# Second part of the conditioning as row sums on VectorE, with the loads, the second z unit and the first fox product reordered

## Chip, cores, metric

One core of one Trainium2 chip. The metric is the device time of the program in microseconds (us), the median of several executions. The engines are TensorE (PE, with its weight loads PEld), VectorE (DVE), ScalarE (ACT), GpSimd (POOL) and SyncE (SP), which here only issues loads.

## The reference

One decoder layer on 256 tokens of width 1024, all in float32. What matters here:

```
mod = (c @ w_ada + b_ada).reshape(B, 6, D)        # w_ada is 1024 x 6144
h = rms_norm(x, g1) * (1 + sc1) + sh1
dn_qkv, dn_z, dn_b, dn_a, fx_qkv, fx_f, gate_a, gate_b = split(h @ w_in)
y_a = (rms_norm(gated_delta_rule(...)) * silu(dn_z)) @ w_o_delta
y_b = forgetting_attention(...) @ w_o_fox
x = x + gt1 * ((sigmoid(gate_a) * y_a + sigmoid(gate_b) * y_b) @ w_out)
h2 = rms_norm(x, g2) * (1 + sc2) + sh2
x = x + gt2 * moe_ffn(h2, ...)                     # 32 experts, top 4
```

`mod` is a product of one row, `c`, with a matrix of 24 MB, called the conditioning below. It is used in three parts of two vectors each: part 0 (sh1, sc1) at the start, part 1 (gt1, sh2) and part 2 (sc2, gt2) after the mixers.

## The kernel before

Every weight before the experts passes through a ring of 8 slots of 1 MB in SBUF. The list UNITS gives the order of the units of 1 MB; unit n goes to slot n % 8, and SP issues its load as soon as unit n - 8 has been used. SP takes the list in order, so a unit whose slot isn't free holds back all behind it. Names: `ada0`, `ada1`, `ada2` are the three parts of the conditioning (8 units each), `dn` the DeltaNet projections (6), `fqk` q and k of the fox attention (4), `fv` its v (2), `z` (2), `gates` (8), then the output matrices.

A projection unit of `w_in` (from `dn` 1 on) is split into a rounded high part and a low part, half a unit (m = 0, 1) at a time: ACT copies the high part (L1130, `split_hi`), POOL subtracts to get the low part (L1846), and PE multiplies in three passes (`three_passes`). ACT splits two units ahead of the one that it takes out of PSUM: in `take(name, u)` the split of a later unit stands in front of the copy of this one, so `fv` 0 is split ahead of the copy of `fqk` 2, of the exponential `exg` (L1196) and of the split of `fv` 1. HI_BUF gives two buffers in turn for the high parts. For `fv` PE waits for both halves before it starts.

The conditioning is computed in two ways. Parts 0 and 1: PE multiplies each unit by `c`, repeated over 32 columns (`ada`, 4 products of 512 columns a unit), and a unit counts as used when PE is done with it. Part 2 (SUMMED): DVE adds the rows weighted by `c` (`add_rows`, L1428 for k = 0, L1431 for the others), each unit being added onto the sum that stands in the unit before; then PE adds over the 128 partitions with 4 products (`ada_over_rows`). There unit k counts as used only when the sum k + 1 is done (`ada_added`), since that sum reads it. Both leave a row in a PSUM bank, which DVE copies (`take_mod_rows`, L1406), PE transposes (`mod_transposes`, L531 to L538), and DVE adds to the biases (`take_mod`, L1390 to L1397).

PE's order around the change is: `fqk` 3, sums of squares for k, `fv` 0 and 1, transposes of k (L704) and of v (L710), `z` 0 and 1, the pair products k k and k q (`chunk_pairs`, 64 x 64), the 8 units of `ada(1, 5)`, `mod_transposes(1, 6)`, transposes of the first inverse (L727), `gates` 0, and five levels of inversion between the halves of `gates` 1 to 5. Then follows the recurrence over four chunks, in which fox products (`fox_branch`) fill gaps, and `fox_branch(2)` behind it, which waits until DVE has taken the first fox group (`take_yb(0)`, L1625). DVE's order is: convolutions of the six `dn` units, small vectors, four pairs of forget-gate masks (L1482, L1484, `rowF_taken`), normalising q and k (L1494, L1496), decays (L1503, L1504), the copies kbx, kd, vb (L1515), the pair products' matrix (L1531), level 0 (L1537), first inverse (L1542).

Of the kernel before, what the change touches and what calls it, by code (L numbers as in the profile page):

```python
# [15 lines left out]
ALU = mybir.AluOpType  # L16
# [24 lines left out]
def layer_kernel(nc, x, c, w_ada, b_ada, g_norm1, w_in, conv_w, a_log, dt_bias, g_onorm, b_fgate,  # L41
# [3 lines left out]
    KD = D // P  # L45
# [18 lines left out]
    W = H * HD  # L64
    COL_Z = QKV
    COL_SMALL = COL_Z + W
    COL_FOX = COL_SMALL + 2 * H
# [4 lines left out]
    with ExitStack() as ctx:  # L72
# [17 lines left out]
        def S(name):  # L90
            if name not in sems:
                sems[name] = ctx.enter_context(nc.semaphore(name))
            return sems[name]
# [160 lines left out]
        def bank(b, a=0, n=512):  # L254
            return ps[:, b, a:a + n]
# [13 lines left out]
        def ada_part(part, ks=range(KD)):  # L269
            return [(f"ada{part}", k, ada_unit(part, k)) for k in ks]  # L270

        def win_part(name, col, us):
            return [(name, u, win_unit(col + 256 * u)) for u in us]

        UNITS = ada_part(0) + win_part("dn", 0, range(6))
        UNITS += win_part("fqk", COL_FOX, range(4)) + win_part("fv", COL_FOX + 2 * W, (0, 1))
        UNITS += win_part("z", COL_Z, (0, 1)) + ada_part(1)
        UNITS += win_part("gates", COL_GATES, range(5)) + ada_part(2, range(3))
        UNITS += win_part("gates", COL_GATES, range(5, 8)) + ada_part(2, range(3, KD))
        UNITS += [("wo_fox", u, rows_unit(w_o_fox, 256 * u, 2)) for u in range(2)]  # L280
# [1 line left out]
        UNITS += [("w_out", u, rows_unit(w_out, 256 * u, 2)) for u in range(4)]  # L282
        NUNITS = len(UNITS)
        UNIT_AT = {(name, i): n for n, (name, i, _) in enumerate(UNITS)}
        SUMMED = (2,)
        SUMMED_NAMES = [f"ada{part}" for part in SUMMED]
        USED_AT = {}
        for name, i, _ in UNITS:
# [215 lines left out]
        def _(pe):  # L504
# [12 lines left out]
            def ada(part, b, ks=range(KD)):  # L517

                for k in ks:
                    w = unit_arrived(pe, f"ada{part}", k)  # L520
                    for q in range(4):
                        last = mm(ps[32 * q:32 * q + 32, b, :], cb[:, k, :], w[:, 512 * q:512 * q + 512],
                                  k == 0, k == KD - 1)
                    last.then_inc(S("unit_used"), 1)
# [102 lines left out]
            def project(name, u, ms=(0, 1)):  # L627


                n = nproj[0]  # L630
                b = n % 2
                if (name, u) in SPLIT:
                    last = project_split(name, u, ms)
                    if ms[-1] == 1:
                        last.then_inc(S("unit_used"), 1)
                        nproj[0] += 1
                    return
                w = unit_arrived(pe, name, u).rearrange("p (k n) -> p k n", k=KD)
                if ms[0] == 0 and n >= 2:
                    bank_free(n)  # L640
                for m in ms:
                    for k in range(KD):
                        if n == 0 and m == 0 and k % 4 == 0:
                            pe.wait_ge(S("hT_low" if k == 0 else "hT_high"), 1)
                        lhsT, rhs = w[:, k, m * P:(m + 1) * P], (hT_first if n < WHOLE else hT)[:, k, :]
                        last = mm(bank(b, m * T, T), lhsT, rhs, k == 0, k == KD - 1)
                if ms[-1] == 1:
                    last.then_inc(S("unit_used"), 1)
                    nproj[0] += 1
# [58 lines left out]
            for t in range(TT):  # L708
                for h in range(H):
                    last = pe.transpose(bank(3 + t, h * P, P), vT[:, h, t * P:(t + 1) * P], ident)  # L710
            last.then_inc(S("tok_ps"), 1)
            project("z", 0)
            project("z", 1)

            pe.wait_ge(S("tok_taken"), 1)
            chunk_pairs((2, 7), kn, kn).then_inc(S("pairs_ps"), 1)
            pe.wait_ge(S("tok_taken"), 2)
            pe.wait_ge(S("unit_qk"), 1)
            chunk_pairs((3, 4), kn, qn).then_inc(S("pairs_ps"), 1)
            pe.wait_ge(S("rowF_taken"), 1)  # L720
            ada(1, 5)
            mod_transposes(1, 6)

            pe.wait_ge(S("X1_ready"), 1)
# [639 lines left out]
        def _(dve):  # L1364
# [69 lines left out]
            for u in range(6):  # L1434
                dve.wait_ge(S("unit_used"), USED_AT[("dn", u)])
                for back in range(4):
                    for m in (2 * u, 2 * u + 1):
                        w = vec("conv", 12 * (3 - back) + m)
                        drawn = bank(u % 2, (m % 2) * T, T - back)
                        if back == 0:  # L1440
                            last = TS(qkv[:, m, :], drawn, w, None, ALU.mult)
                        else:
                            last = STT(qkv[:, m, back:T], drawn, w, qkv[:, m, back:T], ALU.mult, ALU.add)
                    if back < 3:
                        link(last)
                last.then_inc(S("conv_ready"), 1)
            dve.wait_ge(S("conv_ready"), 6)

            dve.wait_ge(S("small_ps"), 2)
# [30 lines left out]
            for h in range(H):  # L1480
# [3 lines left out]
                last = STT(fox_e1[:, h, :], bank(b, a, T), cums[:, 2, 1, H + h:H + h + 1], em("fox_open", 2 * P),  # L1484
                           ALU.subtract, ALU.add)
            last.then_inc(S("rowF_taken"), 1)
            dve.wait_ge(S("rowF_taken"), 1)

            for half in range(2):
# [34 lines left out]
            for t in range(TT):  # L1524
                last = per_head(vb[:, t], 3 + t, beta[:, t, :])
            last.then_inc(S("tok_taken"), 1)
            dve.wait_ge(S("pairs_ps"), 1)
            dve.wait_ge(S("decay_ready"), 1)
            for t in range(TT):
# [18 lines left out]
                last = TTn(attn_t[:, t], bank(3 + t).rearrange("p (h n) -> p h n", h=H), dec_a[:, t], ALU.mult)  # L1548
            last.then_inc(S("attn_ready"), 1)
            TTn(qn, qn, exg, ALU.mult).then_inc(S("qd_ready"), 1)  # L1550
            take_mod_rows(1, 5)
            take_mod(1, 6)
            dve.wait_ge(S("U1_ps"), 1)
            CP(Um[:, 0], bank(2).rearrange("p (h n) -> p h n", h=H))
# [1 line left out]
            for s in range(1, LEVELS):  # L1556
# [30 lines left out]
                if s == 3:  # L1587
# [3 lines left out]
                    TTn(fox_p1, fox_p1, fsum[:, 1, :].unsqueeze(2).to_broadcast([P, H, T]), ALU.mult).then_inc(  # L1591
                        S("fox_p_ready"), 1)

            add_rows(2, 3)
            dve.wait_ge(S("M_ready"), LEVELS - 1)
            dve.wait_ge(S("uw_ps"), 1)
# [2 lines left out]
            for n in range(NCH):  # L1599
                t, r = n // 2, (n % 2) * CH  # L1600
                rows = slice(r, r + CH)
                if n > 0:
                    dve.wait_ge(S("ws_ps"), n)
                    TTn(vnew[rows, t], u_sb[rows, t], ps[rows, 2, :].rearrange("p (h n) -> p h n", h=H),
                        ALU.subtract).then_inc(S("vnew_ready"), 1)
                if n < 2:
                    add_rows(2, 4 + 2 * n)
                if n < NCH - 1:
                    dve.wait_ge(S("ds_ps"), n + 1)
                    if n == 0:  # L1610
                        last = CP(state, bank(7).rearrange("p (h n) -> p h n", h=H))
                    else:
                        for h in range(H):
                            last = STT(state[:, h, :], state[:, h, :], eg[:, h, n:n + 1], bank(7, h * P, P),
                                       ALU.mult, ALU.add)
                    last.then_inc(S("state_ready"), 1)
                    if n < 2:
                        add_rows(2, 5 + 2 * n)
                    dve.wait_ge(S("state_ready"), n + 1)
            take_mod_rows(2, 6)  # L1620

            def take_yb(g):
                dve.wait_ge(S("yb_ps"), g + 1)
                gb_ms = gates[:, 8 + 2 * g:10 + 2 * g, :]
                TTn(gb_ms, bank(g % 2).rearrange("p (m n) -> p m n", m=2), gb_ms, ALU.mult).then_inc(S("yb_taken"), 1)  # L1625

            take_yb(0)
            take_yb(1)
            take_mod(2, 6)
            STT(A2_runs, A2_runs, 1.0, run_vecs[:, 8:12, :].rearrange("p r k -> p (r k)"), ALU.add, ALU.mult)  # L1630
# [286 lines left out]
```

## Time and profile before

| | us |
|---|---|
| median of 3 runs | 1228.27 (1225.92 to 1231.68) |
| the profiled execution | 1225.72 |
| its span, first to last instruction | 1223.9 |
| PE busy in the span | 1130.1 |
| DVE, ACT, POOL busy | 337.1, 185.5, 108.8 |

The time of the profiled execution is 1.8 us more than its span. The change lies in the first 256 us; from about 300 us on the experts run. Times in the rows below are us from the start of the span.

### The profile page before, as it was taken

To read this page: it belongs to the slowest core of one execution; us is meant where nothing else is said; L and a number is where in the kernel's file an instruction comes from. 1 tells how busy PE (TensorE), PEld (TensorE's weight loads), DVE (VectorE), ACT (ScalarE), POOL (GpSimd) and SP (SyncE) were. 2 spreads that over 40 slices of the span, in tenths; PEclk is the share of its full clock that TensorE was granted. 3 is DMA by queue.
4 is the path that set the end of the run, shared out by engine and by line. 5 is a ranking of instruction groups with operands and counts; after the bars stand their busy time and mean duration, and the time that the engine had idled before them with its cause. 6 is when DMAs were issued, how large, how long until landed. Compare 5 with 4: busy or idle time off the path is not lost.

```text
span 1223.9 us, 15032 instructions
## 1 busy us (share of the span) xinstructions
PE 1130.1 (92%) x6251; PEld 582.7 (48%) x6251; DVE 337.1 (28%) x682; ACT 185.5 (15%) x317; POOL 108.8 (9%) x50
## 2 busy tenths in 40 slices
PE   5999999999999999988989889999999999989886
PEld 2999799878433434433333333333433433333322
DVE  1633557341422121321221212122122312212102
ACT  2465344001200000100000000000001000000002
POOL 0764444020000000000000000000000000000000
PEclk9999999999999999999999999999999999999999
DMA  9973765498999999999999999999999999999995
GB/s 352 340 224 103 241 238 207 132 369 333 418 421 428 427 428 428 428 428 428 428 428 428 428 428 428 428 428 428 428 429 428 428 428 428 428 428 428 428 427 245
DMA packets 62559, 464.71 MB, mean 380 GB/s; under 512 B 8469, under 2 KB 31130, under 8 KB 34618
## 3 DMA queue, kind: packets, MB, share of 16 engines
q1 hardware_dynamic: 61688, 462.92, 92.0%
q10 hardware_dynamic: 786, 1.14, 0.3%
q8 instruction: 26, 0.43, 0.1%
q0 software_dynamic: 48, 0.13, 0.0%
q14 instruction: 11, 0.09, 0.0%
HBM read 463.13 MB, written 1.05 MB: 379 GB/s over the span
## 4 chain that ended last, share of the span: by engine, by line
PE 68%; DMA 24%; issue 2%; DVE 2%; ACT 2%; SPq 0%; POOL 0%; DVEq 0%; ACTq 0%
PE ps L506 65%; DMA ring<-in_w_down_dram 12%; DMA ring<-in_w_gate_up_dram 6%; DMA kept<-in_w_down_dram 4%; DMA ring<-in_w_ada_dram 2%; PE ps L973 1%; ACT kept L1324 1%; POOL w_lo L1846 0%; PE ps L1005 0%; ACT w_hi L1130 0%; SPq L350 0%; DVE ring L1537 0%; DVE ring L1531 0%; PE ps L533 0%; DVE kept L1406 0%
## 5 line engine op out<-in xcount | busy, mean ns | idle before, releaser
L506 PE MATMUL ps<-ring,kept 128*64 128x512 f32 (+2 forms) x2984 | 651.3, 599 | 34.8 <-DMA ring<-in_w_down_dram 17.7
L506 PEld LDWEIGHTS ps<-ring,kept 128*64 128x64 f32 (+2 forms) x2984 | 210.5, 138 | 449.5 <-issue 397.0
L506 PE MATMUL ps<-kept 128*128 128x128 f32 (+4 forms) x984 | 192.2, 408 | 8.3 <-ACT kept L1324 3.3
L506 PEld LDWEIGHTS ps<-kept 128*128 128x128 f32 (+2 forms) x984 | 108.3, 176 | 94.5 <-issue 81.8
L1320 ACT ACTIVATE kept<-kept 128x512 f32<-128x512 f32 x32 | 20.2, 630 | 727.7 <-DVE kept L1748 727.7
L1748 DVE TENSOR_SCALAR kept<-ps 128x512 f32<-128x512 f32 x32 | 22.1, 692 | 385.9 <-PE ps L506 385.9
L1770 DVE TENSOR_TENSOR kept<-ps,kept 64x512 f32<-64x512 f32 x64 | 44.1, 689 | 293.8 <-PE ps L506 292.8
L1846 POOL TENSOR_TENSOR w_lo<-ring,w_hi 128x1024 fp32r<-128x1024 f32 x38 | 94.6, 2508 | 107.4 <-ACT w_hi L1130 107.4
L506 PE MATMUL ps<-hT_hi,w_hi 128*128 128x256 f32 x272 | 78.5, 289 | 0.4 <-POOL w_lo L1846 0.4
L506 PE MATMUL ps<-hT_lo,w_hi 128*128 128x256 f32 x272 | 76.9, 283 | 0.0
L506 PE MATMUL ps<-hT_hi,w_lo 128*128 128x256 f32 x272 | 76.8, 282 | 0.0
L506 PE MATMUL ps<-ring 64*64 64x64 f32 (+6 forms) x784 | 73.3, 267 | 1.5 <-DVE ring L1625 1.5
L506 PEld LDWEIGHTS ps<-ring 64*64 64x64 f32 (+3 forms) x784 | 64.1, 157 | 9.9 <-DVE ring L1625 2.4
L506 PE MATMUL ps<-kept,ring 128*128 128x256 f32 (+1 forms) x252 | 56.4, 381 | 4.0 <-DVE kept L1470 2.1
L506 PEld LDWEIGHTS ps<-kept,ring 128*128 128x128 f32 x252 | 47.3, 196 | 11.8 <-issue 3.3
L506 PEld LDWEIGHTS ps<-hT_hi,w_hi 128*128 128x128 f32 x272 | 52.0, 191 | 1.1 <-POOL w_lo L1846 0.6
L506 PEld LDWEIGHTS ps<-hT_lo,w_hi 128*128 128x128 f32 x272 | 52.0, 191 | 0.1
L506 PEld LDWEIGHTS ps<-hT_hi,w_lo 128*128 128x128 f32 x272 | 52.0, 191 | 0.0
L1130 ACT ACTIVATE w_hi<-ring 128x1024 fp32r<-128x1024 f32 x38 | 39.2, 1053 | 48.2 <-PE ps L506 36.9
L973 PE MATMUL ps<-kept 128*128 128x128 f32 x128 | 21.7, 292 | 22.6 <-issue 22.6
L973 PEld LDWEIGHTS ps<-kept 128*128 128x128 f32 x128 | 19.1, 206 | 33.4 <-issue 29.5
L1324 ACT ACTIVATE kept<-ps 128x512 f32<-128x512 f32 x32 | 19.1, 598 | 85.6 <-PE ps L973 85.6
(231 smaller groups left out, 536.5 us busy)
## 6 DMA issues: line engine op xcount, KB each, us to landing
ring<-in_w_gate_up_dram SPq DMA_DIRECT2D x127, 2048.0 KB, 27.6
ring<-in_w_down_dram SPq DMA_DIRECT2D x47, 2048.0 KB, 23.5
kept<-in_w_down_dram SPq DMA_DIRECT2D x16, 2048.0 KB, 24.5
ring<-in_w_ada_dram SPq DMA_DIRECT2D x24, 1024.0 KB, 7.1
ring<-in_w_in_dram SPq DMA_DIRECT2D x22, 1024.0 KB, 10.1
ring<-in_w_out_dram SPq DMA_DIRECT2D x4, 1024.0 KB, 13.7
ring<-in_w_o_fox_dram SPq DMA_DIRECT2D x2, 1024.0 KB, 6.3
ring<-in_w_o_delta_dram SPq DMA_DIRECT2D x2, 1024.0 KB, 7.7
```

Of the source, the lines that this page charges most:

```text
L506: return pe.matmul(dst, lhsT, rhs, start=start, stop=stop, skip_group_check=True)
L973: last = pe.transpose(bank(7, kk * P, P), fours[:, kk, :], ident)
L1130: A(hi_buf_r(n)[:, :, cols], w[:, :, cols], ACT.Copy).then_inc(S("split_hi"), 1)
L1320: A(sig_a, gate_a, ACT.Sigmoid, scale=ALPHA).then_inc(S("sig_ready"), 1)
L1324: A(act_t_last if par == 0 and not more else act_t, bank(7), ACT.Copy).then_inc(S("act_t_ready"), 1)
L1748: TS(gate_a, bank(4), LIMIT, None, ALU.min).then_inc(S("gate_up_taken"), 1)
L1770: TTn(ypair[par * 64:par * 64 + 64, d * 512:(d + 1) * 512], ps[64 * d:64 * d + 64, b, :], gt2_row[64 * d:64 * d + 64, d * 512:(d + 1) * 51 ...
L1846: pool.tensor_tensor(lo_r[:, :, cols], lo[:, :, cols], hi_buf_r(n)[:, :, cols].bitcast(F32), ALU.subtract).then_inc(S("split_lo"), 1)
```

## The change

Part 1 of the conditioning joins part 2 in SUMMED: 8 `add_rows` on DVE and one `ada_over_rows` on PE in place of 8 units of `ada(1, 5)`. Sums 0 to 2 stand behind the convolutions of `dn` 3, 4 and 5; sums 3 to 7 stand behind the masks that end in `rowF_taken`. The list UNITS is reordered, with the `ada1` units among and ahead of the `fqk` units, and `fv` and `z` behind them. On PE, `ada_over_rows(1, 5)` stands ahead of `z` 0, and `z` 1 behind the pair products. On DVE, `take_mod_rows(1, 5)` moves ahead of the pair products' matrix, and `take_yb(0)` into the recurrence, behind the state of the third chunk.

```diff
-        UNITS += win_part("fqk", COL_FOX, range(4)) + win_part("fv", COL_FOX + 2 * W, (0, 1))
-        UNITS += win_part("z", COL_Z, (0, 1)) + ada_part(1)
+        UNITS += ada_part(1, (0, 1)) + win_part("fqk", COL_FOX, (0, 1)) + ada_part(1, (2, 3))
+        UNITS += win_part("fqk", COL_FOX, (2,)) + ada_part(1, (4,)) + win_part("fqk", COL_FOX, (3,))
+        UNITS += ada_part(1, (5, 6, 7)) + win_part("fv", COL_FOX + 2 * W, (0, 1)) + win_part("z", COL_Z, (0, 1))
...
-        SUMMED = (2,)
+        SUMMED = (1, 2)
...
             last.then_inc(S("tok_ps"), 1)
+            ada_over_rows(1, 5)
             project("z", 0)
-            project("z", 1)
...
             chunk_pairs((3, 4), kn, qn).then_inc(S("pairs_ps"), 1)
-            pe.wait_ge(S("rowF_taken"), 1)
-            ada(1, 5)
+            project("z", 1)
             mod_transposes(1, 6)
...
                 last.then_inc(S("conv_ready"), 1)
+                if u >= 3:
+                    add_rows(1, u - 3)
...
             last.then_inc(S("rowF_taken"), 1)
+            for k in range(3, KD):
+                add_rows(1, k)
...
             last.then_inc(S("tok_taken"), 1)
+            take_mod_rows(1, 5)
             dve.wait_ge(S("pairs_ps"), 1)
...
             TTn(qn, qn, exg, ALU.mult).then_inc(S("qd_ready"), 1)
-            take_mod_rows(1, 5)
             take_mod(1, 6)
...
                     if n < 2:
                         add_rows(2, 5 + 2 * n)
+                    else:
+                        take_yb(0)
                     dve.wait_ge(S("state_ready"), n + 1)
             take_mod_rows(2, 6)
...
-            take_yb(0)
             take_yb(1)
```

Three places of the order. First SP's queue behind the small loads (`ring<-in_w_ada_dram` is a unit of the conditioning, `ring<-in_w_in_dram` a projection unit; `unit_used` is PE done with a unit, `ada_added` a sum done). Before:

```order
L350 DMA ring<-in_w_in_dram 128x8x256 [waits unit_used] x8
L350 DMA ring<-in_w_ada_dram 128x2048 [waits unit_used] x8
L350 DMA ring<-in_w_in_dram 128x8x256 [waits unit_used] x5
L350 DMA ring<-in_w_ada_dram 128x2048 [waits unit_used] x3
L350 DMA ring<-in_w_in_dram 128x8x256 [waits unit_used] x3
```

And now:

```order
L351 DMA ring<-in_w_ada_dram 128x2048 [waits unit_used] x2
L351 DMA ring<-in_w_in_dram 128x8x256 [waits unit_used] x2
L351 DMA ring<-in_w_ada_dram 128x2048 [waits unit_used] x2
L351 DMA ring<-in_w_in_dram 128x8x256 [waits unit_used]
L351 DMA ring<-in_w_ada_dram 128x2048 [waits unit_used]
L351 DMA ring<-in_w_in_dram 128x8x256 [waits ada_added]
L351 DMA ring<-in_w_ada_dram 128x2048 [waits ada_added]
L351 DMA ring<-in_w_ada_dram 128x2048 [waits unit_used] x2
L351 DMA ring<-in_w_in_dram 128x8x256 [waits ada_added] x2
L351 DMA ring<-in_w_in_dram 128x8x256 [waits unit_used]
```

The sixth row is `fqk` 3, the seventh `ada1` 5, the eighth `ada1` 6 and 7, the ninth `fv` 0 and 1, the tenth `z` 0. The loads of `fv` 0 and 1, which stood fifth and sixth of the first eight and waited for PE's use of `dn` 2 and 3, now stand behind all of `ada1`, and wait for the sums 3 and 4.

Second DVE, from the last pair of masks on, now:

```order
L1484 SCALAR_TENSOR_TENSOR kept<-ps,kept,ring 128x128
L1486 SCALAR_TENSOR_TENSOR kept<-ps,kept,ring 128x256
L1431 SCALAR_TENSOR_TENSOR ring<-ring,kept 128x2048 [waits ada_added,slot_in3]
L1431 SCALAR_TENSOR_TENSOR ring<-ring,kept 128x2048 [waits ada_added,slot_in5]
L1431 SCALAR_TENSOR_TENSOR ring<-ring,kept 128x2048 [waits ada_added,slot_in7]
L1431 SCALAR_TENSOR_TENSOR ring<-ring,kept 128x2048 [waits ada_added,slot_in0]
L1431 SCALAR_TENSOR_TENSOR ring<-ring,kept 128x2048 [waits ada_added,slot_in1]
L1498 SCALAR_TENSOR_TENSOR ring<-ring 128x1024 [waits qk_rstd,rowF_taken]
L1500 TENSOR_TENSOR ring<-ring 128x1024 [waits qk_rstd]
```

Before, the row of L1498 (then L1494) followed the masks at once; five sums now stand between them.

Third PE, behind the transposes of k and v (L705 and L711, before L704 and L710), now:

```order
L705 MATMUL ps<-kept,ring 128x128 x7
L711 MATMUL ps<-kept,ring 128x128 [waits exg_ready,dec_ready]
L711 MATMUL ps<-kept,ring 128x128 x7
L507 MATMUL ps<-ring,kept 32x512 [waits ada_added]
L507 MATMUL ps<-ring,kept 32x512 x3
```

and, behind `z` 1, which ends with three passes of the last k:

```order
L507 MATMUL ps<-hT_lo,w_hi_54 128x256
L507 MATMUL ps<-hT_hi,w_lo_62 128x256
L532 MATMUL ps<-kept 128x12 [waits run_in,mod_rows_sb]
L532 MATMUL ps<-kept 128x12
L534 MATMUL ps<-kept 128x128 x4
L539 MATMUL ps<-kept 128x64 x4
L727 MATMUL ps<-kept,ring 128x128 [waits X1_ready]
```

The 32 products of 512 columns that stood ahead of the first of these transposes (L531 before) are gone; four of them stand behind L711, and `z` 1 is what PE does ahead of the transposes.

## Rows read from the trace of the kernel before

**Rows 1.** The page: span, and GB/s in 40 slices of the span.

```profile
span 1223.9 us, 15032 instructions
...
GB/s 352 340 224 103 241 238 207 132 369 333 418 421 428 427 428 428 428 428 428 428 428 428 428 428 428 428 428 428 428 429 428 428 428 428 428 428 428 428 427 245
```

**Rows 2.** Chain that ended last, 100 to 150 us: start, us, what.

```profile
124.57 12.62 PE ps L506 x128
...
137.21 2.17 DVE ring L1531 x8
...
139.41 1.30 DVE ring L1537 x2
...
145.68 0.61 DVE kept L1406
```

**Rows 3.** Timeline of PE, 108 to 150 us: start, us, what, idle before.

```profile
109.37 0.47 PE L506 MATMUL ps<-w_hi,hT_hi 128*128 128x256 f32 x1
...
123.48 1.09 PE L710 MATMUL ps<-kept,ring 128*128 128x128 f32 x8 [1.37 <-DVE ring L1504]
...
136.01 2.08 PE L506 MATMUL ps<-ring 128*64 128x64 f32 x64
138.03 7.07 PE L506 MATMUL ps<-ring,kept 128*32 128x512 f32 x64
146.34 0.41 PE L531 MATMUL ps<-kept 12*128 12x12 f32 x2 [1.24 <-DVE kept L1406]
...
147.88 1.09 PE L727 MATMUL ps<-kept,ring 128*128 128x128 f32 x8
```

**Rows 4.** Timeline of DVE.

```profile
102.86 0.47 DVE L1484 SCALAR_TENSOR_TENSOR kept<-ps,kept,ring 128x256 f32<-128x256 f32 x1
116.80 1.23 DVE L1494 SCALAR_TENSOR_TENSOR ring<-ring 128x1024 f32<-128x1024 f32 x1 [13.47 <-ACT ring L1207]
...
178.29 3.52 DVE L1537 TENSOR_TENSOR ring<-ring 128x512 f32<-128x512 f32 x2 [0.84 <-PE ps L506]
...
195.41 4.82 DVE L1431 SCALAR_TENSOR_TENSOR ring<-ring,kept 128x2048 f32<-128x2048 f32 x2
```

**Rows 5.** DMA issues from 166 to 171 us, and from 176 to 181 us: count, size, us to landing.

```profile
ring<-in_w_in_dram SPq DMA_DIRECT2D x1, 1024.0 KB, 5.3
...
ring<-in_w_in_dram SPq DMA_DIRECT2D x1, 1024.0 KB, 6.4
```

**Rows 6.** Timeline of ACT, 108 to 116 us.

```profile
108.09 2.00 ACT L1130 ACTIVATE w_hi<-ring 128x1024 fp32r<-128x1024 f32 x2 [8.87 <-PE ps L506]
110.00 0.58 ACT L1164 ACTIVATE ring<-ps 128x512 f32<-128x512 f32 x1
...
115.63 2.01 ACT L1207 ACTIVATE ring<-ring 128x1024 f32<-128x1024 f32 x2
```

**Rows 7.** Timeline of POOL.

```profile
77.36 2.39 POOL L1846 TENSOR_TENSOR w_lo<-ring,w_hi 128x1024 fp32r<-128x1024 f32 x1 [3.54 <-ACT w_hi L1130]
...
178.83 5.21 POOL L1846 TENSOR_TENSOR w_lo<-ring,w_hi 128x1024 fp32r<-128x1024 f32 x2 [4.02 <-ACT w_hi L1130]
...
198.02 4.42 POOL L1846 TENSOR_TENSOR w_lo<-ring,w_hi 128x1024 fp32r<-128x1024 f32 x1 [3.91 <-ACT w_hi L1130]
```

**Rows 8.** Windows: length, busy of each engine (instructions), granted clock, DMA.

```profile
32.30:36.20 3.90, 3.87 (x9) 3.19 (x10) 1.29 (x1) 3.49 (x5) 0.00 (x0) 0.50 1.10 352
36.20:41.00 4.80, 4.80 (x23) 4.20 (x23) 4.77 (x3) 3.01 (x4) 4.66 (x2) 1.00 1.10 348
90.60:92.70 2.10, 0.03 (x2) 0.05 (x1) 2.03 (x4) 2.10 (x3) 1.62 (x1) 1.00 0.52 98
...
94.20:97.60 3.40, 3.40 (x17) 3.40 (x17) 0.21 (x1) 1.72 (x2) 3.40 (x2) 0.50 0.16 67
```

**Rows 9.** Timeline of PE at the end of the recurrence.

```profile
245.47 1.07 PE L506 MATMUL ps<-ring,kept 128*32 128x512 f32 x8
248.07 3.72 PE L506 MATMUL ps<-ring 128*128 128x256 f32 x16 [1.54 <-DVE ring L1625]
```

More of the change, by code:

```diff
@@ L1592, in _, with take_yb @@
                         S("fox_p_ready"), 1)
+            def take_yb(g):
+                dve.wait_ge(S("yb_ps"), g + 1)
+                gb_ms = gates[:, 8 + 2 * g:10 + 2 * g, :]
+                TTn(gb_ms, bank(g % 2).rearrange("p (m n) -> p m n", m=2), gb_ms, ALU.mult).then_inc(S("yb_taken"), 1)
             add_rows(2, 3)
@@ L1618, in _ @@
                         add_rows(2, 5 + 2 * n)
+                    else:
+                        take_yb(0)
                     dve.wait_ge(S("state_ready"), n + 1)
             take_mod_rows(2, 6)
[L1622 to L1625, printed above, removed]
-            take_yb(0)
             take_yb(1)
```

## The prediction

> **What bounds the kernel now.** I read the page first [rows 1]: from the eleventh slice on (306 us) the core moves up to 428 GB/s without a break, so the experts run at the rate of their loads. These loads are released by PE's products at the end of the mixers, so a shift of the mixers' end moves all that follows by the same. I therefore sum up shifts of PE before 256 us and take them over to the end one to one.
>
> Next the chain [rows 2]. PE holds it nearly everywhere. Between 137.2 and 146.3 us it leaves PE: the pair products release DVE, which makes the matrix (2.17), level 0 (1.30) and more, and takes the conditioning's row last (145.68, 0.61). PE's timeline shows what PE did meanwhile [rows 3]: from 138.03 it ran 7.07 us of `ada(1, 5)`, which DVE's work covers in full, and it waited 1.24 us more for the row. So removing 7.07 us of PE work alone gives nothing there; putting `z` 1 in its place does.
>
> Then who feeds PE from 103 us on. DVE ends the masks at 102.86 + 0.47 = 103.3 and idles 13.47 us, until ACT's L1207 [rows 4]; the five sums now stand in that hole. ACT splits `fv` 1 at 108.09 (`fv` 0 long before) and PE starts `fv` 0 at 109.37 without a wait [rows 3, 6].
>
> **The change, part by part.**
>
> *PE's stretch from L710's end to L727.* Before, 147.88 - (123.48 + 1.09) = 23.3 us [rows 3]. Now `ada_over_rows` (1.07, as the same four products of part 2 [rows 9]), `z` 0, pair products (2.1), `z` 1, transposes of the conditioning (147.88 - 146.34 = 1.5). A `z` unit takes (136.01 - 124.57) / 2 = 5.7 [rows 3]. Sum 1.1 + 5.7 + 2.1 + 5.7 + 1.5 = 16.1. DVE's path behind the first pair products up to the first inverse is 2.17 + 1.30 and a further pair of that length, 4.8 us [rows 2], less than `z` 1, so it is covered. Term: -7.2. Without that cover it would cost the rest of 4.8 us.
>
> *Sums 0 to 2 behind the convolutions.* A sum is 4.82 / 2 = 2.4 us [rows 4]. They hold POOL back by up to a sum each, but POOL has caught up with its work and waits 3.54 us for ACT at 77.36 [rows 7]. Term: 0, and up to 1 if POOL's lead is less than that row suggests.
>
> *Sums 3 to 7 and the loads of `fv`.* This is the part that decides. The load of `fv` 0 now needs sum 3 (`ada_added`), and that stands behind the masks: 103.3 + 2.4 = 105.7 at the earliest, four microseconds before PE wants the split unit. A load of this kind takes 5.3 us, or 6.4 in the other row [rows 5]: it lands at 111.0. ACT, which by then stands waiting at this split, needs 1.0 for the first half [rows 6], so POOL could start at 112.0. Now the two engines collide. At 178.83 POOL's two subtractions, 2.4 each, and DVE's two multiplications that started at 178.29 ran in turns: DVE's pair took 3.52 instead of 1.3, POOL's 5.21 instead of 4.8 [rows 4, 7]. At 198.02 a POOL subtraction took 4.42 instead of 2.4, since DVE's second sum ran until 195.41 + 4.82 = 200.2, and POOL ended 2.2 later [rows 4, 7]. By the same pattern: sum 6 ends at 103.3 + 4 x 2.4 = 113.0, POOL's first half at 115.2, sum 7 at 117.6, POOL's second half at 119.8. Then PE starts `fv` 0, not at 109.4. Term: +10.4. Lower bound, without any collision: 112.0 + 4.8 = 116.8, +7.4; upper, with the load at 6.4, +11.5, as the turns hide most of it.
>
> Skill and row on this lock: the Trainium skill (SBUF — State Buffer, "SBUF: two separate sides") says that the pair of ports which VectorE and GpSimd share is an exclusive lock for a whole instruction, taken by a VectorE operation with two SBUF inputs, and that the loser fully blocks. By that rule the term is the +10.4 above, if the waiting engine always comes next, which the page does not say; with shared bandwidth, and no block, it would be near +7.4. The row of 198.02 agrees with the block.
>
> *PE's clock.* PE idles from about 109.7 to 119.8. In the trace, the idle stretch 90.6 to 92.7 is followed by a stretch at the lower granted level (0.50, 1.2 GHz) from 94.2 to 97.6. After the pause near 30 us PE worked from 32.3 to 36.2 at 0.50 and got 9 products done, where the next 4.8 us at 1.00 (2.4 GHz) hold 23 [rows 8]. Half the work of 3.9 us is lost. Term: +1.9; 0 if the clock stays, +3.8 if the low stretch lasts twice as long.
>
> The Trainium skill (TensorE: Matmul & The Clock Gate, "Part 1: The HAM clock gate") calls this ramp less than 1% of a typical span and advises against fitting it. By that advice the term is left out and the result is 1.9 us lower; 1% here is three times the whole shift that I forecast, so I go by the row.
>
> *What is late next.* ACT stands at the split of `fv` 0 and holds back `exg`, the split of `fv` 1 and the roots for q and k. From the split of `fv` 1 to L1207 it takes 115.63 - 108.09 = 7.5 us [rows 6]. That split starts near 116.2, L1207 near 123.8, DVE's decays (L1504, 6.6 us after L1494 [rows 3, 4]) end near 131.5. PE ends `fv` 1 at 119.8 + 11.7 + 1.9 = 133.4, later, so PE remains the bound and its wait of 1.37 us for L1504 [rows 3] goes. Term: -1.4.
>
> *`gates` 0.* Its high part can be copied only after ACT took `z` 1, which now ends just ahead of the transposes: 0.6 + 1.0 + 2.4 for copy, split and subtraction [rows 6, 7], with issue 4.1 us, against 1.5 + 1.1 us of transposes on PE. Term: +1.5 (0 to +3, if DVE's multiplications block POOL too).
>
> *`take_yb(0)` in the recurrence.* PE's wait of 1.54 us at 248.07 goes [rows 9]; DVE has the time for 0.69 us there. Term: -1.5.
>
> Sum: -7.2 + 10.4 + 1.9 - 1.4 + 1.5 - 1.5 = +3.7 us. The profiled execution, 1225.7 us, would become 1229.4. It lies 2.5 us under the median of 1228.27, so against the median I forecast 1232.0.
>
> **The rivals.**
> 1. *The waits cost less*: POOL isn't blocked (-3.0) and PE's clock stays up or drops for a moment (-1.5). For it: the gain terms are sure, 8.7 us of PE waits. Against it: both rows above. Result +3.7 - 4.5 = -0.8: 1227.5. Chance 0.20.
> 2. *Other side: the loads come in time.* `fv` 0 must have landed by 103.6 (109.4 less 1.0 and 4.8 of splits), so be issued by 98.3. Then the terms of `fv`, clock and L1504 vanish: -7.2 + 1.5 - 1.5 = -7.2, 1221.1. Against it: the sum it needs stands behind masks that end at 103.3. The change turns faster than before when PE starts `fv` 0 before about 116. Chance 0.08.
> 3. *A second collision*: the low clock lasts twice as long (+1.9), and POOL is held by DVE at `gates` 0 as at 178.83 (+1.5): +7.1, 1235.4. For it: DVE's attention and q multiplications fall just there. Chance 0.20.
> 4. *The shift is swallowed*: the experts' loads run ahead of the mixers' end and the time stays 1228. Against it: they wait for PE. Chance 0.05.
>
> The forecast itself has 0.47, its own range 1229.5 to 1234.5.
>
> **How the numbers follow.** Range: from rival 1 with a microsecond below it to rival 3 with 2 above, 1226 to 1237.5; rival 2 and half of rival 3's tail stay out. A measurement of this kernel tells 0.5%, 6.1 us, from no change. Faster: rival 2 at its better half and a little of rival 1, 0.08. Slower, over 1234.4: rival 3 and the top of the forecast's range, 0.24. Same: 0.68.
>
> **What would show it.** A PE wait of 7 to 11 us ahead of `fv` 0, released by POOL, and ACT idle before that, until about 111 us, for a load of `w_in`; granted clock 0.50 behind it; five L1431 in a row from 103.3, the last stretched to over 4 us; POOL's first subtraction of `fv` at over 3 us; 16 us from L711 to L727; a PE wait of 1 to 3 us at `gates` 0; none at the third fox group. The forecast is wrong if `fv` 0 is issued before 100 us, if PE has other work at the wait, or if the mixers' end moves and the experts' end does not.

## The result, and the profile after

| | before | after |
|---|---|---|
| median | 1228.84 | 1234.36 |
| lowest to highest | 1225.23 to 1231.68 | 1231.58 to 1236.06 |
| the profiled execution | 1225.72 | 1236.06 |
| its span | 1223.9 | 1233.7 |

The ratio after to before is 1.0049, with a 95% interval of 1.0038 to 1.006: slower by 5.5 us. The interval excludes no change, though the difference is just under the 0.5% that the prediction takes as what a measurement tells. I had forecast 1232.0. The two profiled executions lie near opposite ends of their kernels' times, 3.1 us under the one median and 1.7 over the other, so their difference of 10.3 us is about twice that of the medians. Below I count the difference of the profiles first, and let the experiments' medians say what each cause is worth.

The page of the changed kernel, its span and the busy time of the engines, beside [rows 1]:

```profile
span 1233.7 us, 14934 instructions
...
PE 1132.7 (92%) x6195; PEld 587.1 (48%) x6195; DVE 358.2 (29%) x690; ACT 185.3 (15%) x317; POOL 112.5 (9%) x50
```

DVE has 21 us more work than before, the eight sums. PE has 56 instructions fewer (6195 for 6251; the trace counts two for each of the 28 products of 512 columns that are gone), yet is busy 2.6 us longer, since more of its work runs at the lower clock.

The chain that ended last, from the masks to `gates` 0 (start, us, what), beside [rows 2]:

```profile
103.99 0.39 DVE kept L1486
104.38 2.27 DVE ring L1431
...
106.66 5.54 DMA ring<-in_w_in_dram
...
112.22 1.06 ACT w_hi L1130
...
113.36 7.21 POOL w_lo L1850 x2
...
120.70 13.21 PE ps L507 x96
133.91 0.87 PE ps L705 x8
134.78 0.87 PE ps L711 x8
135.66 14.91 PE ps L507 x168
...
151.08 1.06 ACT w_hi L1130
...
152.21 2.37 POOL w_lo L1850
...
154.72 5.33 PE ps L507 x30
```

Before, PE held this stretch alone, from 92.68 to the decays at 120.84. Now the chain leaves PE at 101.6, for 19 us: the last masks and sum 3 on DVE, the load that waited for it, the first half of the split on ACT, two subtractions on POOL that together took 7.21 us, and then PE. That is the path of the prediction, link by link. A second excursion, of 4.1 us from L1164 at 150.59 to PE at 154.72, stands at `gates` 0.

Who held POOL is seen in the timelines of DVE, ACT and POOL (start, us, what, idle before), beside [rows 4, 6, 7]:

```profile
104.30 14.06 DVE L1431 SCALAR_TENSOR_TENSOR ring<-ring,kept 128x2048 f32<-128x2048 f32 x5
```

```profile
112.22 2.00 ACT L1130 ACTIVATE w_hi<-ring 128x1024 fp32r<-128x1024 f32 x2 [20.56 <-DMA ring<-in_w_in_dram]
```

```profile
113.36 11.87 POOL L1850 TENSOR_TENSOR w_lo<-ring,w_hi 128x1024 fp32r<-128x1024 f32 x4 [21.75 <-ACT w_hi L1130]
```

Five sums took 14.06 us where five times 2.4 is 12.0, and four subtractions 11.87 where four times 2.4 is 9.6: each engine lost about one operation of the other. The last of the five sums took 4.25 us, POOL's first subtraction 2.85 and its second 4.39. The sums end at 118.4, POOL's second subtraction at 120.6.

The same stretch on PE, and the end of the recurrence, beside [rows 3, 9]:

```profile
120.70 0.55 PE L507 MATMUL ps<-w_hi,hT_hi 128*128 128x256 f32 x1 [9.93 <-POOL w_lo L1850]
...
135.59 1.07 PE L507 MATMUL ps<-ring,kept 128*32 128x512 f32 x8
...
152.02 1.09 PE L727 MATMUL ps<-kept,ring 128*128 128x128 f32 x8
...
253.95 3.72 PE L507 MATMUL ps<-ring 128*128 128x256 f32 x16
...
263.08 1.20 PE L855 MATMUL ps<-kept,ring 128*128 128x128 f32 x8 [2.43 <-DVE ring L1519]
264.07 10.43 PE L507 MATMUL ps<-ring 128*128 128x256 f32 x40
```

`fv` 0 starts 11.3 us later than before. From there to the end of the transposes of v it is 135.66 - 120.70 = 15.0 us, where [rows 3] give 15.2. From there to L727 it is 152.02 - 135.66 = 16.4 where it was 23.3. `fox_branch(2)` starts without a wait at 253.95, 5.9 us later. Then comes what I had not forecast: PE waits 2.43 us ahead of L855, and the 40 products behind it take 10.43 us. In the kernel before the wait was shorter and the products faster:

```profile
255.17 1.09 PE L855 MATMUL ps<-kept,ring 128*128 128x128 f32 x8 [0.40 <-DVE ring L1515]
256.10 8.90 PE L506 MATMUL ps<-ring 128*128 128x256 f32 x40
```

What holds DVE ahead of L855 is one small product (L1635 makes `A2`, 8 numbers a row), in the timelines of DVE and POOL of the changed kernel:

```profile
259.05 0.17 DVE L1634 SCALAR_TENSOR_TENSOR kept<-kept 128x8 f32<-128x8 f32 x1
259.13 2.33 DVE L1635 SCALAR_TENSOR_TENSOR kept<-kept 128x8 f32<-128x8 f32 x1
```

```profile
259.09 2.35 POOL L1861 TENSOR_TENSOR bias_r<-kept,bias_hi 32x1024 fp32r<-32x1024 f32 x1
```

L1635 starts 0.04 us after POOL's subtraction of the bias and ends with it; its twin L1634, just ahead, took 0.17. In the kernel before the pair of products (there L1630 and L1631) came only at the tail of the same subtraction, which ends at 253.44:

```profile
253.17 0.31 DVE L1630 SCALAR_TENSOR_TENSOR kept<-kept 128x8 f32<-128x8 f32 x1
```

```profile
251.08 2.36 POOL L1857 TENSOR_TENSOR bias_r<-kept,bias_hi 32x1024 fp32r<-32x1024 f32 x1
```

DVE's pair came 5.9 us later with the change and POOL's subtraction 8.0, so the two now meet from the start of the subtraction.

The windows with a low granted clock (length, busy of each engine, granted clock, DMA), beside [rows 8]:

```profile
93.30:100.10 6.80, 6.80 (x30) 6.44 (x30) 0.21 (x1) 0.00 (x0) 0.00 (x0) 0.50 0.00 0
...
120.70:124.00 3.30, 3.30 (x15) 3.30 (x16) 0.00 (x0) 3.27 (x6) 3.30 (x2) 0.50 1.10 348
...
154.80:158.10 3.30, 3.30 (x16) 3.30 (x17) 0.00 (x0) 1.46 (x2) 3.30 (x2) 0.50 0.03 7
264.10:267.30 3.20, 3.20 (x9) 2.54 (x9) 1.41 (x2) 0.00 (x0) 0.00 (x0) 0.50 0.65 159
```

The clock is at 0.50 (1.2 GHz) behind each of the three waits of the changed kernel, of 9.93, 1.6 and 2.43 us; the experiments below show that it needn't fall behind the two short ones. At the first, only 3.3 us of low clock fall on work (it is low from 113.8 already, while PE waits). The first row, 6.8 us long where [rows 8] show 3.4, lies ahead of the first wait of PE that the change makes. It belongs to this execution: in the other nine profiles of this case, three of them of kernels with the changed kernel's code up to there (`A2` later, split earlier, `z` 1 back), the low stretch near 95 us is 3.4 us long.

### The profile page after: what moved, and what is told of

It reads as the page before. It is cut to its first block, busy times and chain, and to the rows that moved or that the text cites. A ratio compares the mean times of both kernels' runs of the same rounds, so it can differ in the third digit from the quotient of the medians.

```text
span 1233.7 us, 14934 instructions
## 1 busy us (share of the span) xinstructions
PE 1132.7 (92%) x6195; PEld 587.1 (48%) x6195; DVE 358.2 (29%) x690; ACT 185.3 (15%) x317; POOL 112.5 (9%) x50
## 4 chain that ended last, share of the span: by engine, by line
PE 68%; DMA 24%; ACT 3%; issue 2%; DVE 1%; POOL 1%; ACTq 0%; SPq 0%; DVEq 0%
PE ps L507 66%; DMA ring<-in_w_down_dram 12%; DMA ring<-in_w_gate_up_dram 6%; DMA kept<-in_w_down_dram 4%; PE ps L973 1%; POOL w_lo L1850 1%; DMA ring<-in_w_in_dram 1%; ACT kept L1324 1%; DMA ring<-in_g_onorm_dram 1%; ACT w_hi L1130 0%; PE ps L1005 0%; PE ps L515 0%; DVE kept L1635 0%; DVE ring L1431 0%; ACT ring L1113 0%
## 5 line engine op out<-in xcount | busy, mean ns | idle before, releaser
L507 PE MATMUL ps<-ring,kept 128*64 128x512 f32 (+2 forms) x2928 | 643.0, 597 | 33.0 <-DMA ring<-in_w_down_dram 17.5
L507 PE MATMUL ps<-kept 128*128 128x128 f32 (+4 forms) x984 | 197.5, 420 | 8.3 <-ACT kept L1324 3.3
L1850 POOL TENSOR_TENSOR w_lo<-ring,w_hi 128x1024 fp32r<-128x1024 f32 x38 | 98.4, 2609 | 111.1 <-ACT w_hi L1130 111.1
L507 PE MATMUL ps<-ring 64*64 64x64 f32 (+6 forms) x784 | 76.2, 272 | 0.0
L507 PEld LDWEIGHTS ps<-kept,ring 128*128 128x128 f32 x252 | 47.1, 195 | 11.6 <-issue 3.3
L1431 DVE SCALAR_TENSOR_TENSOR ring<-ring,kept 128x2048 f32<-128x2048 f32 x14 | 37.1, 2653 | 1.2 <-ACT ring L1251 0.5
```

The lines of the kernel that those rows point to most:

```text
L507: return pe.matmul(dst, lhsT, rhs, start=start, stop=stop, skip_group_check=True)
L1431: last = STT(w, w, vec("c", k), unit_sb(UNIT_AT[(f"ada{part}", k - 1)]), ALU.mult, ALU.add)
L1850: pool.tensor_tensor(lo_r[:, :, cols], lo[:, :, cols], hi_buf_r(n)[:, :, cols].bitcast(F32), ALU.subtract).then_inc(S("split_lo"), 1)
```

## The experiments

Each was measured against the kernel before, on the same chip, the first four on one chip and the last four on another. The kernel before had medians of 1228.41 and 1228.36 there. Each interval is 3 to 5 us wide, so what a single step of 2 or 3 us is due to is read from the traces.

| kernel | median us | ratio to before | 95% interval |
|---|---|---|---|
| after, loads of `fv` ahead | 1233.46 | 1.0037 | 1.002 to 1.0053 |
| before, `take_yb(0)` moved alone | 1228.38 | 0.9998 | 0.9977 to 1.0018 |
| after, `A2` later | 1231.03 | 1.0022 | 1.0006 to 1.0039 |
| after, split of `gates` 0 earlier | 1231.87 | 1.0026 | 1.0009 to 1.0044 |
| after, sums spread out | 1221.55 | 0.9944 | 0.9924 to 0.9964 |
| after, `z` 1 back | 1243.65 | 1.0129 | 1.0111 to 1.0147 |
| all that helped | 1216.75 | 0.9912 | 0.9896 to 0.9928 |
| before, `take_yb(0)` moved, `A2` later | 1226.38 | 0.9986 | 0.9972 to 0.9999 |

### The loads of `fv` ahead of the last two units

```diff
-        UNITS += ada_part(1, (5, 6, 7)) + win_part("fv", COL_FOX + 2 * W, (0, 1)) + win_part("z", COL_Z, (0, 1))
+        UNITS += ada_part(1, (5,)) + win_part("fv", COL_FOX + 2 * W, (0, 1)) + ada_part(1, (6, 7))
+        UNITS += win_part("z", COL_Z, (0, 1))
```

> The changed kernel with one line of the list of units altered: the two fv units stand ahead of ada1 6 and 7, so that their loads wait for PE's use of fqk 0 and 1 (78 and 84 us) and for no sum. Everything else as in the change, the five sums in one place included. Theory (the load of fv is late because it waits for sum 3): fv 0 is loaded before 92 us, PE starts it behind the sums of squares without a wait, the 9.9 us of waiting and the 1.3 us of low clock behind it go, the 1.4 us wait for the decays comes back: 1234.4 - 9.8 = 1224.6, ratio to before near 0.9966. Rival (the wait comes from the sums themselves, which lock GpSimd out, or from ScalarE's order, and not from the load): PE still waits over 5 us at fv 0, time 1229 or more.

Measured 1233.46, so nearly nothing of the 10 us came back. Its timelines of PE, DVE and POOL (this kernel has one line more, so L1431 is L1432 and so on):

```profile
109.80 0.47 PE L508 MATMUL ps<-w_hi,hT_hi 128*128 128x256 f32 x1
...
117.70 0.36 PE L508 MATMUL ps<-w_hi,hT_hi 128*128 128x256 f32 x1 [1.81 <-POOL w_lo L1851]
...
126.41 1.09 PE L706 MATMUL ps<-kept,ring 128*128 128x128 f32 x8 [1.25 <-DVE ring L1501]
130.67 1.97 PE L712 MATMUL ps<-kept,ring 128*128 128x128 f32 x8 [3.17 <-DVE ring L1509]
```

```profile
111.08 8.62 DVE L1432 SCALAR_TENSOR_TENSOR ring<-ring,kept 128x2048 f32<-128x2048 f32 x2 [0.15 <-DMA ring<-in_w_ada_dram]
119.63 3.39 DVE L1499 SCALAR_TENSOR_TENSOR ring<-ring 128x1024 f32<-128x1024 f32 x1
```

```profile
109.65 7.90 POOL L1851 TENSOR_TENSOR w_lo<-ring,w_hi 128x1024 fp32r<-128x1024 f32 x2 [10.91 <-ACT w_hi L1131]
```

The wait for the load was the cause of the 9.93 us: with the load early, `fv` 0 starts at 109.80 without a wait. But the five sums behind the masks are a second, nearly equal bound. They now meet the subtractions of `fv` 1 and `z` (POOL 7.90 for 4.8, the last two sums 8.62 for 4.8), and the two products that normalise q and k, 1.23 and 1.22 in the changed kernel, take 3.39 and 3.41. Three waits of PE, 6.2 us together, stand where there was one of 9.93, and the clock falls with them, for 3.4 us from about 118.7 on and for 6.8 us from about 128.9 on: `z` 0 starts at 134.43 instead of 136.58. My expectation of 1224.6 took the first bound away and forgot the one behind it.

### The third fox group alone, on the kernel before

```diff
                         add_rows(2, 5 + 2 * n)
+                    else:
+                        take_yb(0)
...
-            take_yb(0)
             take_yb(1)
```

> The kernel before with the move of the first fox group alone. Theory (the move removes a PE wait of 1.5 us, but brings VectorE's small product with two SBUF inputs under a GpSimd subtraction of the biases, which blocks it 2.3 us, after which the clock is low): PE waits over 2 us ahead of the transposes of the DeltaNet output, result between +0.5 and +2 us, 1229.3 to 1230.8, ratio 1.0004 to 1.0016. Rival (the collision in the changed kernel is an accident of that one execution): 1.5 us faster, 1227.3, ratio 0.9988.

Measured 1228.38, ratio 0.9998: no change, where I had expected 0.5 to 2 us more; the interval reaches from 2.8 us faster to 2.2 slower. The wait ahead of the third fox group is gone, and the lock appears in its place, in a kernel that has nothing else of the change. Timelines of PE, DVE and POOL:

```profile
256.93 1.09 PE L855 MATMUL ps<-kept,ring 128*128 128x128 f32 x8 [2.24 <-DVE ring L1515]
```

```profile
253.09 2.15 DVE L1630 SCALAR_TENSOR_TENSOR kept<-kept 128x8 f32<-128x8 f32 x1
```

```profile
252.86 2.36 POOL L1857 TENSOR_TENSOR bias_r<-kept,bias_hi 32x1024 fp32r<-32x1024 f32 x1
```

On DVE the `A2` products still start at 253.1, but POOL's subtraction stands 1.8 us later than before, so set against POOL's work DVE reaches them 1.9 us sooner. (All stands later here since the granted clock fell to 0.50 for 3.4 us near 148.7, behind the wait of 1.25 us at L531; in the kernel before it stayed at 1.00 behind that wait.) From `fox_branch(2)` to L855 it is 8.94 us where it was 7.10: the 1.54 us of the wait that went come back as 1.84 us, and low clock can follow. So the traces show the term of -1.5 wrong by all of its size, which the interval alone would not. Nor is it an accident of one execution: in all six profiles that have the move with `A2` in its old place, one of its products is held for 1.91 to 2.33 us and PE waits 1.99 to 2.43 us at L855.

### `A2` behind its row, on both kernels

The two products of L1634 and L1635 move behind `on_ready`, which releases PE's L855; nothing needs them before. The same edit on the changed kernel, and on the kernel before with `take_yb(0)` moved.

```diff
-            STT(A2_runs, A2_runs, 1.0, run_vecs[:, 8:12, :].rearrange("p r k -> p (r k)"), ALU.add, ALU.mult)
-            link(STT(A2, mod[:, 32:40], 1.0, vec("g2", 0, KD), ALU.add, ALU.mult))
...
             last.then_inc(S("on_ready"), 1)
+            STT(A2_runs, A2_runs, 1.0, run_vecs[:, 8:12, :].rearrange("p r k -> p (r k)"), ALU.add, ALU.mult)
+            link(STT(A2, mod[:, 32:40], 1.0, vec("g2", 0, KD), ALU.add, ALU.mult))
```

> The changed kernel with the two small products for A2 moved behind the normalised output of DeltaNet, so that nothing with two SBUF inputs stands between the conditioning's columns and PE's transposes. Theory (port lock by the bias subtraction): PE's wait there falls from 2.4 us to under 0.6 and the low clock behind it goes, 1234.4 - 2.0 - 1.5 = 1230.9, ratio to before near 1.0017. Rival (the wait is for ScalarE's roots or for the fox product): the wait stays and the time is 1234.

> The kernel before with the first fox group taken in the recurrence and the two small products for A2 late. Theory: the move is worth 1.5 us and the wait of 0.4 us for the DeltaNet output once nothing of VectorE falls under the bias subtraction: 1228.4 - 1.9 = 1226.5, ratio near 0.9985. Rival (the move is worth nothing in any surroundings, since another wait follows): 1228.4.

Measured 1231.03 and 1226.38: 3.3 us under the changed kernel's median, and 2.0 us under the kernel before. PE of the second:

```profile
253.10 1.09 PE L855 MATMUL ps<-kept,ring 128*128 128x128 f32 x8
254.03 8.90 PE L506 MATMUL ps<-ring 128*128 128x256 f32 x40
```

No wait, and 40 products in 8.90 us at the full clock again. In the changed kernel the lock takes 2.43 us of wait and, where the clock falls behind it, 10.43 - 8.90 = 1.53 more. L855 starts 2.07 us sooner than in the kernel before. With two tiny products out of POOL's way, the move of `take_yb(0)` is worth its 1.54 us of wait; the other 0.4 is the wait that stood at L855 before, and belongs to `A2`. `A2` later on the kernel before, without the move, wasn't run.

### The split of `gates` 0 ahead of `z` 1's copy

```diff
+            split_hi(BEFORE_GATES, 0)
             take("z", 1)
-            for n in range(BEFORE_GATES, BEFORE_GATES + 2):
-                split_hi(n, 0)
-                split_hi(n, 1)
+            split_hi(BEFORE_GATES, 1)
+            split_hi(BEFORE_GATES + 1, 0)
+            split_hi(BEFORE_GATES + 1, 1)
```

> The changed kernel with ScalarE copying the first half of gates 0 ahead of taking z 1 out of PSUM, instead of behind it. Theory (gates 0 waits because its split starts only when z 1 is done): GpSimd has the low part ready before PE is done with the transposes, the wait of 1.6 us at gates 0 and the low clock behind it (1.4 us) go: 1231.4, ratio near 1.002. Rival (GpSimd is held up by VectorE's products of the attention there): the wait stays within 0.5 us, 1234.

Measured 1231.87, 2.5 us under the changed kernel. POOL's first subtraction of `gates` 0 starts at 149.23 instead of 152.21, and PE goes on from the transposes of L727 (at 152.34) without a wait:

```profile
153.19 0.36 PE L507 MATMUL ps<-hT_hi,w_hi 128*128 128x256 f32 x1
```

In the changed kernel it goes on at 154.72, 1.6 us after the end of L727, and with a low clock for 3.3 us. The lock at L855 is still there, with a wait of 2.10 us.

### The sums spread out

On top of the loads of `fv` ahead, sum 3 stands ahead of DVE's wait for `e8_ready`, sums 4 and 5 behind `cums_taken`, and 6 and 7 where all five stood.

```diff
+            add_rows(1, 3)
             dve.wait_ge(S("e8_ready"), 1)
...
             dve.wait_ge(S("cums_taken"), 1)
+            for k in (4, 5):
+                add_rows(1, k)
...
-            for k in range(3, KD):
+            for k in range(6, KD):
                 add_rows(1, k)
```

> e1 (fv loaded ahead of ada1 6 and 7) with the sums taken apart: sum 3 ahead of VectorE's wait for the exponential near 80 us, sums 4 and 5 behind the copy of the cumulated gates near 95 us, sums 6 and 7 behind the masks. Theory (in e1 the lateness of the load was replaced by the port lock between the five sums, the split of fv 1 and z, and the normalising of q and k): GpSimd's two halves of fv 1 are ready by 115.9, VectorE normalises at 117 to 119, PE waits at most 1.5 us for the decays, nothing at fv: 1234.4 - 9.8 = 1224.6, ratio to before near 0.9966. Rival (the sums as such cost, wherever they stand, since a sum of 2.4 us always falls on some subtraction): 1230 to 1233 as in e1.

Measured 1221.55, 6.8 us faster than before and 3 us better than I had expected. The sums on DVE:

```profile
79.77 4.50 DVE L1432 SCALAR_TENSOR_TENSOR ring<-ring,kept 128x2048 f32<-128x2048 f32 x1
94.70 7.61 DVE L1432 SCALAR_TENSOR_TENSOR ring<-ring,kept 128x2048 f32<-128x2048 f32 x2
104.84 4.79 DVE L1432 SCALAR_TENSOR_TENSOR ring<-ring,kept 128x2048 f32<-128x2048 f32 x2
```

They are held as hard as before (4.50 for one, 7.61 for two), but in holes where nobody waits for DVE, and the last two are done at 109.6, before POOL's next work matters. `fv` 0 starts at 109.16, and the transposes of v at 123.27, where the kernel before has 123.48. So the cost of the sums was their place. The -7.2 of the stretch behind them is left over at L728 (L727 before), and 5.9 us of it at L856 (L855 before); the medians' 6.8 has an interval of 4.4 to 9.3. Whether the early load is needed with it was not tried apart; sum 3, for which the load of the changed kernel waited, now stands near 80 us anyway.

This execution also has the wait of 1.6 us at `gates` 0 and one of 2.05 at L856 (L855 before), and behind neither does the clock fall: from 249.2 to 252.6 us it is 1.00, and at `gates` 0 too (windows, as above):

```profile
143.40:146.80 3.40, 3.38 (x28) 3.40 (x29) 0.00 (x0) 1.55 (x2) 3.40 (x2) 1.00 0.02 7
```

### `z` 1 back ahead of the pair products

```diff
             project("z", 0)
+            project("z", 1)
...
             chunk_pairs((3, 4), kn, qn).then_inc(S("pairs_ps"), 1)
-            project("z", 1)
```

> The changed kernel with z 1 back ahead of the pair products. Theory (z 1 covers VectorE's 4.8 us between the pair products and the first inverse, but its late end is what makes gates 0 wait): PE waits 2.3 us ahead of the transposes of the first inverse, the 1.6 us at gates 0 and the low clock behind it go, within 1 us of the changed kernel, 1233.5 to 1235.5. Rival (the cover is worth its full 4.8 us and the wait at gates 0 is independent of it): 1238 or more.

Measured 1243.65, 9.3 us slower than the changed kernel, as the rival said and not the theory. PE, DVE and POOL:

```profile
162.41 1.97 PE L727 MATMUL ps<-kept,ring 128*128 128x128 f32 x8 [9.32 <-DVE ring L1547]
```

```profile
150.67 2.16 DVE L1536 SCALAR_TENSOR_TENSOR ring<-ps,kept,ring 128x128 f32<-128x128 f32 x8 [7.63 <-PE ps L507]
152.86 4.00 DVE L1542 TENSOR_TENSOR ring<-ring 128x512 f32<-128x512 f32 x2
156.90 5.46 DVE L1547 TENSOR_TENSOR ring<-kept,ring 128x512 f32<-128x512 f32 x2
```

```profile
151.20 10.62 POOL L1850 TENSOR_TENSOR w_lo<-ring,w_hi 128x1024 fp32r<-128x1024 f32 x4 [10.12 <-ACT w_hi L1130]
```

I had priced only the cover, the 4.8 us of DVE's path less the transposes that remain. The products of level 0 and of the first inverse fall under POOL's four subtractions for `gates` 0 and 1 and take 4.00 and 5.46 us; after POOL is done, the same pair at 162.39 took 1.29. So `z` 1 between the pairs and L727 does two things: it gives PE something to do, and it lets DVE end before POOL starts (in the changed kernel DVE is done at 148.5, and POOL starts at 152.2).

### All that helped

The spread sums, the later `A2` and the earlier split together.

> e5 with the two small products for A2 late (e3) and the first half of gates 0 copied ahead of taking z 1 (e4). Theory (the three places are independent, each gave its own time back): 1224.6 - 3.4 - 2.5 = 1218.7, ratio near 0.992. Rival (one of the waits hides another): above 1222.

Measured 1216.75, 11.6 us faster than the kernel before and 17.6 faster than the changed one. PE:

```profile
140.71 1.09 PE L728 MATMUL ps<-kept,ring 128*128 128x128 f32 x8
...
245.32 1.09 PE L856 MATMUL ps<-kept,ring 128*128 128x128 f32 x8
```

L728 (L727 before) starts 7.2 us sooner than in the kernel before, L856 (L855) 9.9 us sooner (the two profiled executions differ by 9.7), with no wait ahead of either `gates` 0 or L856.

## Why the prediction was right, and where it was not

The time came out 5.5 us above that of before, where I had +3.7, for the reasons given, with one term wrong and one too small. The stated range of 1226 to 1237.5 held no change at all too, so that the time fell into it proves little; the links of the chain and the experiments do. Part of the sum is luck: `fv` 0.5 us and the clock with L1504 0.7 us below the forecast stand against 1.5 and 1.0 us above it at the two terms that failed.

- **PE's stretch, -7.2.** 16.4 us against 16.1 forecast, so -7.0. The spread sums show it with little else: 140.72 against 147.88 at L727.
- **Sums 0 to 2, 0.** Two subtractions at 67.93 took 6.40 us for 4.8; POOL still waited 2.42 us for ACT at 76.76. Right.
- **`fv` and the sums, +10.4.** Issue at 106.66 (forecast 105.7), landing 112.20 (111.0), PE's start 120.70 (119.8). PE's wait was 9.93 us. The late 0.9 us comes with the masks, which are themselves 1.0 us late. PE was ready for `fv` 0 at 120.70 - 9.93 = 110.8, 1.4 later than before, so the change's own part is 11.3 - 1.4 = 9.9. The profiles of the three other kernels with this order show the same wait, 9.92 to 9.93 us. The turns of DVE and POOL were as read from the rows of 178.83 and 198.02 (only the first subtraction, 2.85 us, was under the 3 us of my sign). What I did not see is that the sums' place suffices without the late load, as the first experiment shows; the load alone, landed at 112.20 and with 1.1 and 4.8 us of splits behind it, would by these rows still cost 7.3 us, which is an estimate. So the rival in which the loads come in time would not have given 1221.1, but about 1233; with the sums moved too it is 1221.55. Its condition named one bound where there were two.
- **Clock +1.9 and L1504 -1.4.** `fv` took 13.21 us, against the 11.7 that the prediction gives it: +1.5. The wait of 1.37 us for the decays went. Together the stretch from `fv` 0 to the end of L711 came out 0.2 us shorter, forecast +0.5. But the size of the clock's part differs between executions. With the split earlier `fv` took 13.07 us; with `A2` later and with `z` 1 back, which have the same code up to there, it took a good 14 us, with the clock low until 127 instead of 124:

```profile
120.53 14.45 PE ps L507 x96
```

```profile
120.79 14.30 PE ps L507 x96
```

Over the four profiles the term is 1.4 to 2.8 us, 2.1 in the mean, and the whole stretch +0.3.
- **`gates` 0, +1.5.** The wait was 1.6 us. The low clock that can follow it was left out. Here it cost 1.5 us: PE comes to its first product of 128 columns 7.33 us after it goes on, at 162.05, where it takes 5.83 us with `A2` later. The experiment that removes the stall gives back 2.5 us, so the term is about 1.0 too small, as far as an experiment with an interval of over 4 us can tell. In the profiles with `A2` later, with `fv` ahead and with the sums spread, the same wait of 1.6 us has no low clock behind it, so the 1.0 would be an average over executions that have it and ones that don't.
- **`take_yb(0)`, -1.5.** This is the term that failed. The wait went as forecast, and one of 2.0 to 2.4 us at L855 took its place 9 us later, with 1.5 us of low clock behind it in four of six profiles. Alone the move measured 0; with `A2` out of the way the two edits measured -2.0 (interval -3.4 to -0.1), 1.5 of it the move's by the trace. I had asked whether DVE had time for 0.69 us there, and not what DVE's next instructions would meet.

With each term as measured the sum is -7.0 + 9.9 - 0.2 + 2.5 + 0 = 5.2 us, and the medians differ by 5.5; with the mean of the four profiles for `fv` it is 5.7. About 0.4 us of the 5.5 lies outside the span and in no term: a run's time is 2.26 us more than its span in the changed kernel and 1.85 in the kernel before. No run shows why; with `A2` later it is 1.84 again.

Of the rivals, the first fails in both halves: POOL was blocked and the clock fell. The second's condition didn't come about, with the load issued at 106.66. Of the third, the low clock behind the wait for `fv` 0 took no second stretch of work in the changed kernel's profile, but it did in two of the three other profiles with this order; POOL wasn't held at `gates` 0 (its first subtraction took 2.37). Another part of its price came from a place where POOL holds DVE. The fourth is refuted by the kernels that move the mixers' end far: with `z` 1 back L855 starts 8.9 us later than in the changed kernel, and the time is 9.3 us longer; in the last kernel L856 starts 9.9 us sooner than L855 before, and the profiled execution is 9.7 us shorter.

The Trainium skill (SBUF — State Buffer, "SBUF: two separate sides") says that the loser of the shared pair of ports blocks for the whole instruction. The traces agree: 2.33 us for a product of 128x8 that takes 0.17 when POOL is quiet. The Trainium skill (TensorE: Matmul & The Clock Gate, "Part 1: The HAM clock gate") puts the ramp penalty under 1% of a typical span and advises against fitting a count of cold products. Here one stretch costs 1.5 us, 0.12% of the span, which agrees as a share; but it is a quarter of what the change did, so for small changes the measurement decides against the advice.

The difference of the two profiles, 10.3 us, isn't fully explained. Up to the end of the 40 products behind L855 PE is 9.5 us late; some 1.4 us of it is there before `fv` 0 is due. The longer low clock at 93.3 us can explain it in this execution only: in the three other profiles with this order that stretch is 3.4 us, and PE is still 1.2 to 1.9 us later than before, while with the sums spread it is 0.2 us early. Where that comes from stays open.

## What to carry to other kernels

When DVE work with two SBUF inputs is put into a hole of DVE, ask what POOL does in that hole and what either engine is asked for next. The length of the hole isn't enough: five sums in one hole of 13.5 us cost about 10 us, and the same five in three holes, with the loads ahead, showed no cost. Where an edit brings an engine forward by a microsecond, follow its next few instructions too, the tiny ones included. When a wait has a releaser, look for the bound that stands just behind it before promising the whole wait; and count a PE wait of even 1.3 us with up to another 1.5 us of clock.

## What I had not expected of the hardware

- The lock is blind to size. A product of 8 elements a partition took 2.33 us under a POOL subtraction over 32 partitions (0.17 when free); two products of 512 elements took 4.00 and 5.46 us instead of 1.29.
- DVE operations that read one tensor from PSUM and one from SBUF (and a column of factors in SBUF) weren't held: the eight of L1536 at 150.67 took 2.16 us while POOL subtracted from 151.20 on, the same as in [rows 2], where they took 2.17.
- A short wait is a gamble on the clock. Behind PE's wait of 1.6 us at `gates` 0 the granted clock fell to 0.50 for 3.3 us in the changed kernel, and stayed at 1.00 behind the same wait with `A2` later, with `fv` ahead and with the sums spread. Behind the wait at L855 it fell at 2.43, 2.24, 2.10 and 1.99 us and stayed at 2.05 and, with `fv` ahead, at 2.43, so the length of the wait doesn't decide it. Behind the wait of 1.25 us at L531 it fell with `take_yb(0)` moved alone and stayed in two profiles with the same code there. Behind the wait of 2.1 us that ends near 92 to 94 us it fell, within 3 us, in all ten profiles. Behind the long wait for `fv` 0 it was low in all four profiles looked at (the changed kernel, `A2` later, the split earlier, `z` 1 back). What decides it at the short ones these runs don't show.
